# Differential attention on one core: the vector engine's order of combining, maxima and head copies is written anew

## The reference

```python
def _diff_attend(qb, q_pos, kh, vh, k_pos, lam):
    s = jnp.einsum('bhcqd,bhckd->bhcqk', qb, kh)
    mask = k_pos[None, :] <= q_pos[:, None]
    p = jax.nn.softmax(jnp.where(mask, s, -jnp.inf), axis=-1)
    pd = p[:, :, 0] - lam * p[:, :, 1]
    return jnp.einsum('bhqk,bhkv->bhqv', pd, vh)
...
    o = o * lax.rsqrt(jnp.mean(o * o, axis=-1, keepdims=True) + EPS) * subln.astype(f32)
```

## Time and profile before

| | |
|---|---|
| time, median of 3 runs | 3694.91 us (3688.51 to 3695.05) |
| time of the profiled execution | 3692.8 us |
| its span | 3691.0 us |
| TensorE busy | 3574.9 us (97%) |
| VectorE busy | 1788.5 us (48%) |
| ScalarE busy | 1259.5 us (34%) |
| GpSimd busy | 1481.8 us (40%) |
| first and last head copy (L1930) start at | 1048.2 and 1123.2 us |

### The profile page before, as it was taken

One profiled execution on the slowest core, in us unless ns is written; L12 is line 12 of the kernel. 1 busy time (PEld: TensorE's weight loads), 2 busy tenths in 40 slices (PEclk: granted clock), 3 DMA queues, 4 the chain that ended last, 5 costly groups with the idle time before them and its releaser, 6 DMA issues.

```text
span 3691.0 us, 54789 instructions
## 1 busy us (share of the span) xinstructions
PE 3574.9 (97%) x20604; PEld 3069.1 (83%) x20604; DVE 1788.5 (48%) x2371; ACT 1259.5 (34%) x2107; POOL 1481.8 (40%) x649
## 2 busy tenths in 40 slices
PE   8999999999988999999999999999999998899998
PEld 8988999999966888888887888888888876588886
DVE  3773664447555444532246442335232588753234
ACT  3643332222264222422243532234222443642222
POOL 3341444443302444444442234443444475044443
PEclk9999999999998999999999999999999999999999
DMA  4221222222201222222232112232322221022222
GB/s 147 77 75 33 86 89 89 89 92 81 88 22 46 97 92 97 86 91 97 92 108 75 52 58 95 93 106 83 97 91 97 92 81 68 7 95 94 97 95 83
DMA packets 86428, 307.38 MB, mean 83 GB/s; under 512 B 9568, under 2 KB 11872, under 8 KB 86112
## 3 DMA queue, kind: packets, MB, share of 16 engines
q1 hardware_dynamic: 85824, 303.69, 24.9%
q10 hardware_dynamic: 416, 1.05, 0.1%
HBM read 302.60 MB, written 2.10 MB: 83 GB/s over the span
## 4 chain that ended last, share of the span: by engine, by line
PE 84%; DVE 10%; ACT 3%; DVEq 2%; issue 1%; DMA 0%; POOL 0%; ACTq 0%; SPq 0%; POOLq 0%
PE psum L372 69%; PE psum L584 6%; DVE psum L2747 1%; PE psum L602 1%; DVE psum L2767 1%; DVE arena L1168 1%; PE psum L622 1%; PE psum L2095 1%; DVE arena L1199 1%; DVEq L2740 1%; PE psum L1306 1%; PE psum L1324 0%; DVE scale L664 0%; PE psum L2059 0%; ACT arena L2616 0%
## 5 line engine op out<-in xcount | busy, mean ns | idle before, releaser
L335 POOL TENSOR_TENSOR w_lo<-w_raw,w_hi 128x1024 fp32r<-128x1024 f32 (+1 forms) x507 | 1262.9, 2491 | 1879.6 <-ACT w_hi L323 1879.6
L323 ACT ACTIVATE w_hi<-w_raw 128x1024 fp32r<-128x1024 f32 (+1 forms) x507 | 534.7, 1055 | 1818.0 <-PE psum L372 1805.7
L372 PE MATMUL psum<-x_hi,w_hi 128*128 128x512 f32 (+1 forms) x2744 | 903.0, 357 | 11.9 <-POOL w_lo L335 7.9
L372 PE MATMUL psum<-x_lo,w_hi 128*128 128x512 f32 (+1 forms) x2744 | 903.8, 358 | 0.0
L372 PE MATMUL psum<-x_hi,w_lo 128*128 128x512 f32 (+1 forms) x2744 | 899.2, 356 | 0.0
L372 PE MATMUL psum<-y_hi,w_hi 128*128 128x264 f32 (+1 forms) x2272 | 632.8, 328 | 11.7 <-DVE arena L1177 3.4
L372 PE MATMUL psum<-y_lo,w_hi 128*128 128x264 f32 (+1 forms) x2272 | 633.3, 328 | 0.0
L372 PE MATMUL psum<-y_hi,w_lo 128*128 128x264 f32 (+1 forms) x2272 | 630.9, 327 | 0.0
L372 PEld LDWEIGHTS psum<-x_hi,w_hi 128*128 128x128 f32 x2744 | 486.4, 189 | 95.7 <-POOL w_lo L335 9.4
L372 PEld LDWEIGHTS psum<-x_lo,w_hi 128*128 128x128 f32 x2744 | 485.4, 189 | 78.7 <-issue 1.4
L372 PEld LDWEIGHTS psum<-x_hi,w_lo 128*128 128x128 f32 x2744 | 486.2, 189 | 76.4
(11 more groups left out here) (506 smaller groups left out, 4265.6 us busy)
## 6 DMA issues: line engine op xcount, KB each, us to landing
w_raw<-in_weights SPq DMA_DIRECT2D x566, 512.0 KB, 3.3
resid<-in_xT SPq DMA_DIRECT2D x8, 264.0 KB, 7.9
out_dram<-resid SPq DMA_DIRECT2D x16, 128.0 KB, 1.7
arena<-in_lru_w SPq DMA_DIRECT2D x1, 1024.0 KB, 10.0
rope_sb<-in_rope SPq DMA_DIRECT2D x1, 528.0 KB, 11.3
rope_sb<-in_rope ACTq DMA_DIRECT2D x1, 512.0 KB, 4.8
y_space<-in_pool_inv ACTq DMA_DIRECT2D x1, 512.0 KB, 6.9
mats<-in_mats SPq DMA_DIRECT2D x1, 448.0 KB, 10.3
```

The source lines that it names most:

```text
L323: nc.scalar.activation(weight_parts(n, i, c)[0][:, 0:w], RAW[:, (n + c) % 4, 0:w], ACT.Copy).then_inc(high_ready, 1)
L335: nc.gpsimd.tensor_tensor(wl[:, 0:w], RAW[:, (n + c) % 4, 0:w], wh[:, 0:w], ALU.subtract).then_inc(low_ready, 1)
L372: last = mm(o[:, a, :], wt[:, k * P:k * P + P], x[:, k, a * (w // banks):(a + 1) * (w // banks)], start=(k == 0 and p == 0), stop=(k == kt ...
```

## The change

The vector engine's loop is written in another order: in iteration n it now combines unit n first, then takes the maxima of unit n + 2, and then, in a head's u1, copies out the head before. The maxima of unit 1 are taken ahead of the loop. The wait for `c_e` ahead of the maxima is gone, since the combining ahead of them has waited for a later unit's. The maxima have three pairs of columns in place of two.

```diff
-        NEGM = [SM[:, 44 + 2 * i:46 + 2 * i] for i in range(2)]
+        NEGM = [SM[:, a:a + 2] for a in (44, 46, 54)]
...
-                                                bias=NEGM[n % 2][:, c:c + 1], accum_out=total)
+                                                bias=NEGM[n % 3][:, c:c + 1], accum_out=total)
...
             maxima(0)
+            maxima(1)
             dve.wait_ge(st["c_vt"], DT)
             nc.vector.memset(PT_META, 0.0).then_inc(st["c_zero"], 1)
             for n, (h, i) in enumerate(C_UNITS):
-                if n + 1 < len(C_UNITS):
-
-                    if n:
-                        dve.wait_ge(st["c_e"], n)
-                    maxima(n + 1)
-                if i == 1 and h:
-                    head_out(h - 1)
                 w = META + P * (i + 1)
                 dve.wait_ge(st["c_e"], n + 1)
                 nc.vector.reciprocal(RSUM, SUM1[n % 2])
...
                 stt(E0[n % 2][:, 0:w], E1[n % 2][:, 0:w], SHARE, E0[n % 2][:, 0:w], ALU.mult,
                     ALU.add).then_inc(st["c_pd"], 1)
+                if n + 2 < len(C_UNITS):
+                    maxima(n + 2)
+                if i == 1 and h:
+                    head_out(h - 1)
             head_out(C_HEADS - 1)
```

More of the change, by code:

```diff
@@ L1920, in maxima @@
                     bank = score_parts(n, 0)[0][0]
-                    last = nc.vector.reduce_max(NEGM[n % 2], G[:, bank:bank + 2, 0:META + P * (i + 1)], AX.X, negate=True)
+                    last = nc.vector.reduce_max(NEGM[n % 3], G[:, bank:bank + 2, 0:META + P * (i + 1)], AX.X, negate=True)
                 else:
                     for c in range(2):
-                        last = nc.vector.reduce_max(NEGM[n % 2][:, c:c + 1], score_view(n, c), AX.XY, negate=True)
+                        last = nc.vector.reduce_max(NEGM[n % 3][:, c:c + 1], score_view(n, c), AX.XY, negate=True)
                 last.then_inc(st["c_mx"], 1)
```

## The result

| | before | changed |
|---|---|---|
| median | 3692.48 us (12 runs, 3688.51 to 3695.88) | 3700.93 us (12 runs, 3697.99 to 3705.08) |
| ratio | | 1.0022, 95% interval 1.0015 to 1.0029 |
| head of attention | 10.80 us | 11.31 us, or 12.19 where the clock falls in it |

The change makes the kernel 8.4 us slower, 0.22%; by the interval 5.5 to 10.7 us. The profiled execution took 3705.1 us, with a span of 3703.3. It is the slowest of the twelve, so I read durations and waits in it, and take the total from the medians.

What follows compares the result with a forecast made beforehand. A head's 10.80 us was bound by a chain through VectorE, TensorE and ScalarE, VectorE bounding its first 4 us. 7 x 0.48 + 0.30 = 3.66 us on the median 3694.91 gave 3698.6 us, range 3692.0 to 3704.5.

Steps and rivals of the forecast that it cites:

- The order was the same already: VectorE's loop: maxima of n + 2 already stood right behind the combining of n, so they move no earlier.
- The head copy, 0.48 us a head: Heads 1 to 7: copy behind u3's maxima delays u2's transposition by 0.48 us; a head takes 11.28 us.
- TensorE's queue decides: At u2's transposition: TensorE's own queue allows it at 1074.30, the combining at 1074.27; the later counts.
- The wait costs nothing: VectorE's wait for `c_e` ahead of the maxima: removing it gains 0, at most 0.1 us.
- The start, 0.30 us: Loop start: the clearing now delays the first combining and transposition, a loss of 0.30 us, once; bounds 0 and 0.48.
- The likeliest case: Attention loop: only the copy's and the start's delays count, without clock falls; 3698.6 us, chance 0.52.
- the falls: Rival, middle heads: one longer TensorE pause drops its clock to 1.2 GHz; 3702.6 us with four, 3705.6 with seven; chance 0.28.
- the plain delay: Attention loop: seven head copies at 0.48 us plus 0.30 at the start, 3.66 us slower; chance 0.52.
- The rival's price: Each fall of TensorE's clock in a head costs 1.0 us, at most 1.7 and at least nothing.
- around the new pause TensorE is busy without a break: Argument against clock falls in middle heads: TensorE's busy share there is not as low as before 1117.
- the clock falls in this loop behind its longest pause, none behind the short ones: Reading of the earlier trace: clock falls in the last head after 1.31 us idle; middle heads stay at 2.4 GHz.

Runs made afterwards that it cites:

- e1: The changed kernel with the head copy put back ahead of the combining of u1; median 3694.13 us, ratio 0.9998 to the kernel before.
- e5: The changed kernel with `values` of u0 moved on TensorE behind the transposition of u2 in seven heads; median 3699.83 us, ratio 1.0022 to the kernel before.
- e7: The kernel before with only the head copy moved between combining of u1 and maxima of u3, keeping the `c_e` wait and two column pairs; 3696.15 us, ratio 1.0007.
- e3: The changed kernel with the head copy between combining of u1 and maxima of u3, and the clearing ahead of unit 1's maxima again; 3693.31 us, ratio 1.0000.
- e2: The kernel before with only the head copy moved, to behind the maxima of u3; median 3703.27 us, ratio 1.0023.
- e6: The kernel before with only the maxima of unit 1 put ahead of the clearing; 3694.31 us in one run.
- e4: The changed kernel with 12 unused identity transpositions added on TensorE in the pause of each of seven heads; 3697.31 us, ratio 1.0008 to the kernel before.

## Why the prediction was right, and where it was short

**The order was the same already: right.** e1 shows it.

**The head copy, 0.48 us a head: right in mechanism and size.** The measured head is 0.51 longer, and the table above follows the forecast step by step within 0.1 us. The step that costs is the one named: the copy done 2.5 us later (2.6 forecast), `values` of u0 behind it, the next scores and the transposition of u2 behind that. TensorE's queue decides, as forecast, but by 0.2 us and not 0.03: the combining of u2 ends at 1062.85 + 0.63 = 1063.48, and the transposition starts at 1063.74. With TensorE's queue freed, 0.35 remain (e5).

**The wait costs nothing: wrong, by 0.07 us.** I read it where the maxima came right behind the combining and waited for nobody, and there it is free. Where the maxima wait for the mask, a second wait adds 0.07 us (e7 against e3, e2 against the changed kernel). In the changed kernel, without it, this is a small gain, 0.06 a head, that takes a bit off the copy's cost. Against it, from the held-up `values` of u0 to the next mask it took 1.06 us (1062.56 to 1063.62) and not 0.99.

**The start, 0.30 us: mis-sized, and it hangs on the clock.** It is 0.38 where the clock is at 1.2 GHz and nothing where it is at 2.4 (e6), as in the changed kernel's own trace.

**The likeliest case left the clock out of the middle heads: this is what failed in the sum.** The text gave the falls a chance of 0.28 and took the plain delay, 3.66 us, as the likeliest. In the trace the clock falls behind the pause of 1.77 us in every second middle head. The rival's price of 1.0 us a fall measured 0.88, and that "around the new pause TensorE is busy without a break" was no protection. The text also read the kernel before too narrowly: "the clock falls in this loop behind its longest pause, none behind the short ones" overlooks the start, where TensorE runs 6.8 us at 1.2 GHz behind idle pieces of 1.39 and 1.04 us.

What the falls are worth in the total stays open. The six middle heads are 5.73 us longer, 3.06 by the delay and 2.7 by three falls. But the changed kernel's trace has no fall at the start and in the last head, where before's has, so the loop as a whole is only 3.9 us longer, near the 3.66 of the forecast, and the time at 1.2 GHz in it is the same, 10.2 us. In e2, with falls at all three places, the loop is 6.7 us longer. The measured 8.4 has an interval from 5.5 to 10.7, which holds 6.7 and not 3.9. How often the clock falls at each place over twelve executions is not on record, and whether what is left is scatter isn't either. The time came nearer than the loss, and that is luck: 3698.6 was forecast and 3700.9 measured, 2.3 us apart, because the forecast started from a median of three runs, 3694.91, that lies 2.4 us above the one of twelve. The loss was forecast at 3.7 and measured at 8.4.

The Trainium skill ("TensorE: Matmul & The Clock Gate", section "HAM oscillation — how this bites in real kernels") was nearer than my choice in that a long enough pause in every turn of a loop is paid again and again. By that rule all seven heads would fall if the pause is long enough, and none if it isn't. The trace agrees with neither: three of the six middle heads fell, and the others and the last, with the same pause of 1.77 us, kept 2.4 GHz.

## What to carry to other kernels

Before you reorder a loop, write out both instruction streams: here the change in the words ("two units ahead") was none in the stream, and one short copy that moved with it was nearly the whole effect. An instruction that frees a buffer for another engine belongs into the first gap after its input is ready, ahead of long work (in e3 this made a head 0.24 us shorter than before); what it releases, and what is queued behind the released instruction, is its price. And add up the idle pieces of TensorE, not only the delay: two short pauses that become one can cost the clock on top. Before you compare two traces, sum up the time at the lower clock stage by stage: here two thirds of the difference between two executions lay where the programs are the same.

## What the runs showed of the hardware that I had not expected

- In the traces TensorE's clock fell behind pauses of 1.77 us in three of six middle heads (cost 0.88 us each), behind 1.84 us in three of six (e2, 0.91 each) and behind 2.00 us in three of six (e5, 1.3 each), and never in the middle heads of kernels whose longest pause there was 1.1 us (e3 and e7: 1.04 and 1.08 ahead of the transposition of u2). With twelve useless transpositions in the pause there was no fall in six heads.
- The same code fell in one execution and not in another. At the start of the loop, behind idle pieces of 1.39 and 1.04 us, TensorE runs at 1.2 GHz in six of the nine traces from the first scores on, and at 2.4 in the other three. With the fall it takes 15.84 us to the second head (before), without it 14.54 (e7).
- A second semaphore wait on a VectorE instruction seems to cost about 0.07 us when the instruction is held up (0.39 against 0.32 us behind the start of the releasing matmul), and nothing that shows when it isn't (heads of 10.80 us before and in e1).
- The first matmuls of `values` after the pause took 0.46 us where they take 0.39 without one (L1773), at the same granted clock; from their start to that of L1775 it is 0.30 us (1062.56 to 1062.86) against 0.23 (1064.18 to 1064.41). Behind e4's pause of 0.23 us it is 0.46 as well.
